# One decoder layer on one Trainium2 core: another beginning, level products in blocks of 64 tokens, and the last products in halves of columns

## The reference, cut to what matters

```python
n = rmsnorm(h, g_mix)
q, k, v, qi, ki, wi, qb, kb, vb, gb, rb, uc, vc = split_proj(n @ w_in)
o_a = attn_fn(q, k, v, qi, wi, ki)      # indexer scores, top-k keys, softmax over them
o_b, s_b = gla(qb, kb, vb, log_a, s0)   # gated linear attention, in chunks of 64 tokens
h = h + concat(o_a, o_b * silu(rb), o_c) @ w_out
h = h + (silu(n2 @ w_ffn_gate) * (n2 @ w_ffn_up)) @ w_ffn_down
h = h + sigmoid(rmsnorm(h, g_ple) @ w_ple_gate) * (p @ w_ple_proj)
```

```python
att = jnp.einsum('bthk,bshk,btshk->bhts', qc, kc, jnp.exp(diff))   # diff = b[t] - b[s]
```

## Time and profile before

| | before |
|---|---|
| median of 3 runs | 1409.0 us (1406.78 to 1410.85) |
| the profiled execution's own time | 1407.28 us |
| its span (first to last instruction and transfer) | 1405.6 us |
| PE busy | 1393.0 us, 99% |
| DVE busy | 850.4 us, 61% |
| ACT busy | 578.7 us, 41% |
| share of PE in the chain that ended last | 98% |
| granted clock of PE, all 40 slices | 9 of 9 tenths shown |

### The profile page before, as it was taken

How to read it: one execution, slowest core, us unless ns; L and a number is a source line. 1 busy time by engine, 2 the same in 40 slices (tenths; PEclk the granted TensorE clock), 3 DMA queues, 4 the chain that set the end, 5 groups by cost and what they waited for, 6 DMA issues and landing times.

```text
span 1405.6 us, 28379 instructions
## 1 busy us (share of the span) xinstructions
PE 1393.0 (99%) x10632; PEld 1375.3 (98%) x10632; DVE 850.4 (61%) x1175; ACT 578.7 (41%) x696; POOL 118.8 (8%) x178
## 2 busy tenths in 40 slices
PE   7999999999999999999999999999999999999998
PEld 7999989999999999999999999999999999999998
DVE  6668767646876555555554444555555556666554
ACT  6545743565334333333333333333333333335332
POOL 1314105000221000000000000000000001111000
PEclk9999999999999999999999999999999999999999
DMA  8847434446544544544445556444544445556553
GB/s 281 226 154 241 164 123 136 147 130 233 178 155 156 179 165 157 173 158 168 156 147 164 165 163 199 158 168 157 171 157 168 159 131 164 164 164 201 176 161 117
DMA packets 76134, 236.69 MB, mean 168 GB/s; under 512 B 13800, under 2 KB 14456, under 8 KB 75704
## 3 DMA queue, kind: packets, MB, share of 16 engines
q1 hardware_dynamic: 71424, 223.59, 48.3%
q0 software_dynamic: 3776, 11.54, 2.7%
q10 hardware_dynamic: 888, 0.93, 0.2%
HBM read 231.48 MB, written 4.47 MB: 168 GB/s over the span
## 4 chain that ended last, share of the span: by engine, by line
PE 98%; DMA 1%; DVE 1%; SPq 0%; ACT 0%; issue 0%; DVEq 0%
PE acc L495 31%; PE acc L497 31%; PE acc L496 31%; PE px L1611 1%; DMA proj<-in_xT 1%; PE px L1496 0%; PE px L1574 0%; PE px L1555 0%; DMA w_raw<-in_w_in 0%; PE px L495 0%; PE px L497 0%; PE px L496 0%; DVE x_lo L1003 0%; PE px L1680 0%; PE px L1567 0%; PE px L1531 0%
## 5 line engine op out<-in xcount | busy, mean ns | idle before, releaser
L445 DVE TENSOR_TENSOR w_lo<-w_raw,w_hi 128x1024 fp32r<-128x1024 f32 (+3 forms) x446 | 507.7, 1143 | 315.6 <-ACT w_hi L439 307.0
L439 ACT ACTIVATE w_hi<-w_raw 128x1024 fp32r<-128x1024 f32 (+3 forms) x446 | 439.5, 989 | 562.7 <-PE acc L497 551.3
L495 PE MATMUL acc<-n_hi,w_hi 128*128 128x288 f32 x1664 | 492.8, 296 | 0.0
L496 PE MATMUL acc<-n_lo,w_hi 128*128 128x288 f32 x1664 | 490.9, 295 | 0.0
L497 PE MATMUL acc<-n_hi,w_lo 128*128 128x288 f32 x1664 | 489.3, 294 | 0.0
L497 PEld LDWEIGHTS acc<-n_hi,w_lo 128*128 128x128 f32 x1664 | 313.5, 188 | 0.0
L496 PEld LDWEIGHTS acc<-n_lo,w_hi 128*128 128x128 f32 x1664 | 312.4, 188 | 0.1
L495 PEld LDWEIGHTS acc<-n_hi,w_hi 128*128 128x128 f32 x1664 | 311.8, 187 | 0.1
L495 PE MATMUL acc<-x_hi,w_hi 128*128 128x288 f32 x816 | 246.5, 302 | 1.0 <-DVE w_lo L445 1.0
L496 PE MATMUL acc<-x_lo,w_hi 128*128 128x288 f32 x816 | 240.8, 295 | 0.0
L497 PE MATMUL acc<-x_hi,w_lo 128*128 128x288 f32 x816 | 240.1, 294 | 0.0
(11 more groups left out here) (283 smaller groups left out, 861.0 us busy)
## 6 DMA issues: line engine op xcount, KB each, us to landing
w_raw<-in_w_gu SPq DMA_DIRECT2D x176, 512.0 KB, 3.8
w_raw<-in_w_in SPq DMA_DIRECT2D x76, 512.0 KB, 4.3
w_raw<-in_w_down SPq DMA_DIRECT2D x64, 384.0 KB, 3.0
w_raw<-in_w_down SPq DMA_DIRECT2D x64, 320.0 KB, 3.0
w_raw<-in_w_ple SPq DMA_DIRECT2D x32, 576.0 KB, 3.8
w_raw<-in_w_out SPq DMA_DIRECT2D x32, 512.0 KB, 4.2
w_raw<-in_w_in SPq DMA_DIRECT2D x12, 256.0 KB, 6.7
proj<-in_xT SPq DMA_DIRECT2D x4, 576.0 KB, 7.5
```

Source lines behind the costliest of these rows:

```text
L439: nc.scalar.activation(whi[:, slot, 0:kt * P], raw[:, slot, 0:kt * P], ACT.Copy).then_inc(S("w_hi_done"), 1)
L445: nc.vector.tensor_tensor(wlo[:, slot, 0:kt * P], raw[:, slot, 0:kt * P], whi[:, slot, 0:kt * P].bitcast(F32), ALU.subtract).then_inc(S("w ...
L495: nc.tensor.matmul(out, w_h, row_of(m_hi_, k0 + k), start=first and k == 0, stop=False)
L496: nc.tensor.matmul(out, w_h, row_of(m_lo_, k0 + k), start=False, stop=False)
```

## The change

- The beginning: x and the first weights arrive in the order in which they are used, the first eight steps' worth in pieces of two; the gains are loaded through ACT's queue. Tile 0 lies in slots 0 and 2, tile 1 in slots 1 and 3, and both add up in the six-bank buffer `px` and not in `acc`.
- Tile 2 is now a plain row of queries, and `ROW_KI` is tile 3: it is no longer among the rows kept raw, but goes through `keep`. `keep_raw` moves from DVE to ACT. The mean of squares moves from the middle of tile 3 into the first half of tile 4's first chunk. ACT loads the table of the logarithm before it waits for the sum.
- The stages `weights` and the copy of `ROW_KI` wait for `keep` of tile 3 instead of the scaling of the raw rows. `TIMETABLE` is the same.
- The table of biases is multiplied with 128 instead of 32 rows, the added ones zero.
- Levels: products of 64 by 64 tokens where the mask has blocks of 64 (`PARTS`).
- The last tile's input products are made for columns 0 to 143 and then 144 to 287, in two banks.

```diff
-ORDER = (ROW_QI, ROW_QI + 1, ROW_KI, *range(ROW_QI + 2, ROW_QI + 8), *range(ROW_K, ROW_K + 4), *range(ROW_Q, ROW_Q + 8),
+ORDER = (ROW_QI, ROW_QI + 1, ROW_QI + 2, ROW_KI, *range(ROW_QI + 3, ROW_QI + 8), *range(ROW_K, ROW_K + 4), *range(ROW_Q, ROW_Q + 8),
...
-SOURCE = (0, 1, MISC_TILE, *range(2, 8), *range(18, 22), *range(10, 18), *range(22, N_ROWS))
+SOURCE = (0, 1, 2, MISC_TILE, *range(3, 8), *range(18, 22), *range(10, 18), *range(22, N_ROWS))
...
+        BEGIN = [(0, 2, [(0, 0)]), (2, 4, [(1, 0)])] + [(4 * c, 4 * c + 4, [(0, c), (1, c)]) for c in range(1, 4)]
...
-            return weights[:, 2 * t + c // 2, (c % 2) * 4 * P:(c % 2 + 1) * 4 * P]
+            return weights[:, 2 * (c // 2) + t, (c % 2) * 4 * P:(c % 2 + 1) * 4 * P]
...
+            return (S("w_lo_done"), c + t) if c % 2 else (S("quarter_lo"), c + t + 1)
...
+        PARTS = {1: [(0, P, 0)], 2: [(0, 64, 64)], 3: [(0, 64, 0), (64, P, 64)]}
...
+            for k0, k1, parts in BEGIN:
+                sp.dma_start(x_f[:, k0:k1, :], a["xT"][:, k0:k1, :]).then_inc(S(f"x_loaded{k0}"), 16)
+                for t, c in parts:
...
+                        .then_inc(loaded[2 * (c // 2) + t] if c % 2 else S(f"w_quarter{t}{c}"), 16)
...
-            sp.dma_start(relb[:, :], a["rel_bias"]).then_inc(S("consts_loaded"), 16)
+            sp.wait_ge(S("att_zero"), 1)
+            sp.dma_start(relb[0:NBUCKET, :], a["rel_bias"]).then_inc(S("consts_loaded"), 16)
...
-                    sp.wait_ge(S("raw_scaled"), 2)
+                    sp.wait_ge(S("acc_read"), kept(ROW_KI))
...
+            def keep_raw(t):
+                act.wait_ge(S("w_used"), 6 if t == 2 else 3 + t)
+                A(proj[:, ORDER[t], :], acc[:, 1, 0:T] if t == 2 else px[:, t, 0:T], ACT.Copy).then_inc(S("raw_kept"), 1)
+            act.dma_start(gains[:, :, :], a["gains"]).then_inc(S("gains_loaded"), 16)
...
+            for k0, k1, parts in BEGIN:
...
+                for k in range(k0, k1):
...
+                for t, c in parts:
+                    act.wait_ge(loaded[2 * (c // 2) + t] if c % 2 else S(f"w_quarter{t}{c}"), 16)
...
+            split_hi(act, "in", 1, 1)
...
-                split_hi(act, "in", 1, c + 1)
-            split_hi(act, "in", 1, 3)
-            for c in range(2):
-                split_hi(act, "in", 2, c)
+                keep_raw(c)
+                split_hi(act, "in", 1, c + 2)
+            keep_raw(2)
+            split_hi(act, "in", 2, 0)
+            split_hi(act, "in", 2, 1)
+            A(epsw[:, :], ones[:, 0:1], ACT.Ln)
...
+            for k0, k1, parts in BEGIN:
+                for k in range(k0, k1):
...
+                for t, c in parts:
...
+            split_lo(dve, "in", 1, 0)
+            split_lo(dve, "in", 1, 1)
...
-            def keep_raw(t):
-                dve.wait_ge(S("w_used"), 2 * t + 2)
-                V.tensor_copy(proj[:, ORDER[t], :], acc[:, (t + 1) % 2, 0:T]).then_inc(S("acc_read"), 1)
-            split_lo(dve, "in", 1, 0)
-            keep_raw(0)
...
-            split_lo(dve, "in", 1, 1)
-            keep_raw(1)
+            split_lo(dve, "in", 1, 2)
...
-            split_lo(dve, "in", 1, 2)
+            split_lo(dve, "in", 1, 3)
+            split_lo(dve, "in", 2, 0)
...
-            split_lo(dve, "in", 1, 3)
-            keep_raw(2)
-            split_lo(dve, "in", 2, 0)
...
-            dve.wait_ge(S("acc_read"), 3)
-            for first, n in ((ROW_QI, 2), (ROW_KI, 1)):
-                raw_rows = proj[:, first:first + n, :]
-                V.tensor_tensor(raw_rows, raw_rows, rstd[:, :].unsqueeze(1).broadcast_to([P, n, T]), ALU.mult)                    .then_inc(S("raw_scaled"), 1)
-            dve.wait_ge(S("raw_scaled"), 2)
+            dve.wait_ge(S("raw_kept"), 3)
+            raw_rows = proj[:, ROW_QI:ROW_QI + 3, :]
+            V.tensor_tensor(raw_rows, raw_rows, rstd[:, :].unsqueeze(1).broadcast_to([P, 3, T]), ALU.mult)\
+                .then_inc(S("acc_read"), 3)
...
-                dve.wait_ge(S("w_used"), tile_done("ple", i, j))
...
-                    for c, done in ((0, S("y_first")), (half, S("y_ready"))):
-                        link(V.tensor_tensor(tmp3[:, c:c + half], tmp2[:, c:c + half], px[:, j, c:c + half], ALU.mult))
+                    for c, done, mm, count in ((0, S("y_first"), S("first_mm"), 1), (half, S("y_ready"), S("w_used"), tile_done("ple", i, j))):
+                        dve.wait_ge(mm, count)
+                        link(V.tensor_tensor(tmp3[:, c:c + half], tmp2[:, c:c + half], px[:, 2 if c else 1, c:c + half], ALU.mult))
...
+                dve.wait_ge(S("w_used"), tile_done("ple", i, j))
...
-            def group(name, i, j, out, hi_, lo_, ready=lambda k: None, after=lambda q: None):
+            def group(name, i, j, out, hi_, lo_, ready=lambda k: None, after=lambda q: None, between=None):
...
-                    products(out, slot, k0, kt, hi_, lo_, first=q == 0, last=q == n_parts - 1).then_inc(S("w_used"), 1)
+                    at = 0
+                    if between and q == 0:
+                        at = kt // 2
+                        products(out, slot, k0, at, hi_, lo_, last=False)
+                        between()
+                    products(out, slot, k0 + at, kt - at, hi_, lo_, first=q == 0 and not at, last=q == n_parts - 1, at=at)\
+                        .then_inc(S("w_used"), 1)
...
-            tile_free("in", 1, 2, 0)
+            firsts = [(0, 0, 0, 2), (0, 0, 2, 4), (1, 0, 0, 4)] + [(t, c, 4 * c, 4 * c + 4) for c in range(1, 4) for t in range(2)]
+            for t, c, k0, k1 in firsts:
+                out, w_h, w_l = px[:, t, 0:T], quarter(whi, t, c), quarter(wlo, t, c)
+                pe.wait_ge(*quarter_hi(t, c))
+                for k in range(k0, k1):
+                    pe.wait_ge(S("x_hi_ready"), k + 1)
+                    M(out, w_h[:, k % 4 * P:k % 4 * P + P], x_hi[:, k, :], start=k == 0, stop=False)
+                for k in range(k0, k1):
+                    pe.wait_ge(S("x_ready"), k + 1)
+                    M(out, w_h[:, k % 4 * P:k % 4 * P + P], x_lo[:, k, :], start=False, stop=False)
+                pe.wait_ge(*quarter_lo(t, c))
+                for k in range(k0, k1):
+                    ins = M(out, w_l[:, k % 4 * P:k % 4 * P + P], x_hi[:, k, :], start=False, stop=k == KT - 1)
+                if c % 2:
+                    ins.then_inc(S("w_used"), 1)
...
-            def squares_sum(q):
-                if q == 0:
...
-                    mean_squares(0)
-            tile_free("in", 1, 2, 1)
-            group("in", 1, 1, acc[:, 0, 0:T], x_hi, x_lo, after=squares_sum)
+            group("in", 1, 1, acc[:, 0, 0:T], x_hi, x_lo)
+            def squares_sum():
+                pe.wait_ge(S("x_ssq"), 1)
+                pe.wait_ge(S("ones_ready"), 1)
+                mean_squares(0)
...
-                pe.wait_ge(S("raw_scaled"), 2)
+                pe.wait_ge(S("acc_read"), kept(ROW_KI))
...
-                        tq = 1 if m == 1 else tt
...
-                            for e in range(2):
-                                pp = slice(64 * e, 64 * e + 64)
-                                ins = M(px[:, bank + e, 256 * tt + P * r:256 * tt + P * r + P], k_[pp, r, P * tt:P * tt + P],
-                                        q_[pp, r, P * tq:P * tq + P], start=True, stop=True)
+                            for s0, s1, t0 in PARTS[min(m, 3) if m else 3]:
+                                for e in range(2):
+                                    pp, first, tq = slice(64 * e, 64 * e + 64), P * tt, P * (1 if m == 1 else tt)
+                                    at = 256 * tt + P * r + t0
+                                    ins = M(px[s0:s1, bank + e, at:at + s1 - s0], k_[pp, r, first + s0:first + s1],
+                                            q_[pp, r, tq + t0:tq + t0 + s1 - s0], start=True, stop=True)
...
-                tile_free("in", t // 2, 2, t % 2)
-                group("in", t // 2, t % 2, acc[:, (t + 1) % 2, 0:T], x_hi, x_lo, after=lambda q: do(stages, 2 * t + q))
+                if t == NSLOT:
+                    pe.wait_ge(S("raw_kept"), 3)
+                else:
+                    tile_free("in", t // 2, 2, t % 2)
+                group("in", t // 2, t % 2, acc[:, (t + 1) % 2, 0:T], x_hi, x_lo, after=lambda q: do(stages, 2 * t + q),
+                      between=squares_sum if t == NSLOT else None)
...
-            def ple(i, j):
+            def ple(i, j, at_end=False):
...
-                if not isinstance(i, int):
+                if not isinstance(i, int) or i:
...
-                inputs(j)
+                if at_end:
+                    last_inputs()
+                else:
+                    inputs(j)
...
+            def last_inputs():
+                for bank, c0, c1, done in ((1, 0, T // 2, S("first_mm")), (2, T // 2, T, S("w_used"))):
+                    products(px[:, bank, c0:c1], (g0 + 3) % NSLOT, 0, GK - KT, p_hi[:, :, c0:c1], p_lo[:, :, c0:c1], at=KT - parts[0])\
...
```

(58 more changed lines are left out.)

20 lines of the change are left out of this document (7 added, 13 removed).

## The result

| | before | changed |
|---|---|---|
| median of 12 runs | 1407.16 us (1406.56 to 1410.85) | 1410.26 us (1408.59 to 1410.82) |
| profiled execution, own time / span | 1407.28 / 1405.6 us | 1408.59 / 1406.8 us |
| PE busy | 1393.0 us | 1393.0 us |
| mean granted clock of PE | 1.000 | 0.998 |

The ratio is 1.0017, 95% interval 1.0009 to 1.0025: 1.3 to 3.5 us slower, a loss that twelve runs can tell from none, though it is under 0.3%. 1410.26 lies in the range of 1403.0 to 1411.0, but the forecast was 1.6 us faster than before. The profiled execution of the changed kernel is the fastest of its twelve. They form two groups, five at 1408.6 to 1409.2 and seven at 1410.2 to 1410.8; the mean clock doesn't tell them apart (0.997 to 0.999 and 0.997 to 0.998).

A forecast was written before the change was run, and what follows sets the result against it. PE, busy in 1393.0 of 1405.6 us, was taken as the bound. New wait +4.2, start -1.1, tile 2's wait -1.15, levels -3.5, end 0 gave -1.6 us: 1407.4 us against 1409.0, range 1403.0 to 1411.0.

The forecast's parts named there:

- What bounds it: Whole kernel: PE is busy in 1393.0 of 1405.6 us, so any new wait of PE is paid in full.
- the place of the new wait: Stage weights on PE waits for keep of ROW_KI, now tile 3, until 42.35: loss of 4.2 us.
- Levels: Level products: blocks of 64 by 64, four side by side, 14.4 ns apart, gain 3.5 us.
- The rival of two blocks at a time: Level products: only two blocks run together, 28.9 ns apart, gaining 0.2 us: 1410.7 us; chance 0.10.
- the Trainium skill's floor of 25 ns: Level products: starts never closer than about 25 ns, gain 1.1 us: 1409.8 us; chance 0.08.
- End: Last tile's products in two halves of columns: gains nothing, 0.1 us at the most.
- the sum's silence on the clock: The forecast total of -1.6 us held no cost for a fall of PE's clock in the 4.2 us pause.
- the fall as a rival: PE's clock falls in the 4.2 us pause at stage weights, costing 1.65 us more: 1409.1 us; chance 0.22.
- The start: Tiles 0 to 2: earlier products gain 1.1 us, and the wait in tile 2 goes, gaining 1.15 us.
- The first: Tiles 0 and 1: x arrives earlier, so tile 2 starts at 21.4 and not 22.51: gain 1.1 us.
- The second gain: Tile 2: PE's wait between its two chunks goes, as the second is now a plain one: gain 1.15 us.
- The base: Time before the change that the forecast was set against: a median of 1409.0 us.

The follow-up runs named there:

- the levels alone: The kernel before with only the level products in blocks of 64 and nothing else of the change: 1403.38 us against 1407.04, ratio 0.9975.
- the two kernels: The changed kernel, 1410.26 us, and the changed kernel with the level products and the last tile as before, 1413.66 us, ratio 1.0039.

## Why the prediction was wrong

- **What bounds it; the place of the new wait**: right. The new wait came out in full, and it was where `ROW_KI` led, 3.9 us for a forecast of 4.2, `weights` at 42.14 for 42.35.
- **Levels**: right. 3.5 forecast; 3.4 by the trace, 3.7 by the medians of the levels alone; the spacing 15 ns for 14.4. The rival of two blocks at a time (28.9 ns) is out, and so is the Trainium skill's floor of 25 ns (TensorE: Matmul & The Clock Gate, section "Wait — 56ns, not 53.3ns?"): here products of 64 columns started 15 ns apart.
- **End**: right, nothing.
- **The step that failed** is the sum's silence on the clock. The prediction had the fall as a rival at 0.22 and 1.65 us; all twelve runs of the changed kernel have a mean clock of 0.997 to 0.999, and in the profiled one it cost 2.94. The chance was too low: the prediction had one pause of 1 us that had done nothing and PE's rest at the start, placed 4.2 us between them, and left the clock out of the sum. The price was too low, as it was taken from the start, where PE loses 1.65 (in the trace of the levels alone 2.6, so this price isn't fixed either): after the pause the slow stretch lasted from 42.1 to about 48.5, over 6 us. Filling the pause gave 3.3 us back. The Trainium skill's section "HAM oscillation — how this bites in real kernels" (TensorE: Matmul & The Clock Gate), which the prediction cited, has the clock fall in pauses for data, and the two traces with a pause of 3.9 us agree with it (0.50 by its end in both).
- **The start**, forecast at 1.1 and 1.15 us of gain: mis-sized, the second failure. The first came out in one execution (21.56), but the eight other traces of the new beginning have tile 2 at 21.9 to 22.7. In each of the nine it follows 9.6 to 9.7 us behind tile 0's second quarter, which the prediction put at 11.65 from one arrival of x's second four steps (9.28). It started at 11.96 in the changed kernel's trace and at 12.2 to 13.1 in the others: ACT began with these steps at 8.8 in the first and at 9.8 to 10.7 in the others, each time after waiting for the transfer. The second gain, 1.15, rested on a wait that the next trace of the same beginning didn't have. And the transfers behind (chunk 8 after the constants) were not followed: the prediction bound the moved *sum* to PE's place alone (36.0), where in most traces PE also waited 0.2 to 0.6 us for the squares. Forecast 2.25 together; measured 0.2 over the levels alone while these waits stood, and 1.5 with them gone.
- **The base**: the forecast stood on a median of 1409.0 from three runs; twelve runs give 1407.16. The forecast of 1407.4 was so 0.2 above the truer base, and the time lay 2.9 above the forecast. That it lies in the range is luck: the same sum and range, set on 1407.16, give 1405.6 and 1401.2 to 1409.2, and 1410.26 is outside. The base was high by the draw of three runs (1406.8, 1409.0 and 1410.9). Of 54 more runs of the kernel before, beside the experiments, three took 1410.9 to 1411.6 with a mean clock of 0.998, so its clock seems to fall now and then too; where is open, as none of them has a trace.

In sum, from the 1407.2 of before: +3.9 for the wait, +2.9 for the clock, -3.4 for the levels, and for the start -2.2 in the profiled execution (1406.8 less 1405.6 is 1.2), about -0.3 in the medians, which leaves the measured +3.1. Forecast (-1.6) and measured (+3.1) are 4.7 apart: 2.9 is the clock and about 1.9 the start; the wait and the levels together take 0.2 off.

## What to carry to other kernels

Where one engine is 99% busy, follow each row that changes its place to everyone who reads it: one tile moved one place back turned a value that was ready 0.6 us early into a wait of 3.9. A pause of a few microseconds on TensorE can cost more than its length, since the clock may fall in it or just after; here filling it with useless products was 3.3 us cheaper than leaving it, and removing it cheaper still. And a wait seen in one trace is a feature of the kernel only when a second trace has it.

## What the runs showed of the hardware

- The granted clock fell to 0.50 in a pause of 3.9 us (in both traces that have one; in all 17 runs of the two kernels the mean clock is under 1), and in single traces also about a microsecond after the end of a pause of 2.1 or 1.3 us, when small products followed; in the trace with the pause filled it did not. A pause of 1.0 us between full products left it alone, in one trace.
- The clock read less than full for about 6.8 us in both traces with the pause of 3.9, and for about 3.4 after those of 2.1 and 1.3; from `weights` to `index` this cost 2.8 and 1.5 us over the 4.93 with the pause filled. What a fall costs isn't one number.
- How long PE stays slow at the kernel's start varies too: the same 24 first products took 4.85 us in one trace of the old beginning and 5.83 in another.
- Products of 64 by 64 in full precision, in turn on the four quarters of the array, started 15 ns apart. That is about a quarter of the 57.7 ns for which one of them holds its quarter, by the prediction's estimate from the earlier trace rows.
